# Expert loop of a mixture-of-experts layer: another order of the small products around gate/up and down

## What is computed

```python
logits = (t @ router_w + router_b)
top_val, top_idx = lax.top_k(logits, TOP_K)      # 4 of 32 experts for each token
gates = softmax(top_val)
for each expert e, for its tokens:
    g, u = split(x @ w_gu[e] + b_gu[e])          # w_gu[e]: 1024 x 2048
    act = (clip(u, -7, 7) + 1) * (min(g, 7) * sigmoid(1.702 * min(g, 7)))
    y = act @ w_down[e] + b_down[e]              # w_down[e]: 1024 x 1024
    out[token] += gate * y
```

## Time and profile before

| | |
|---|---|
| runs | 1322.9, 1323.15, 1326.55 us; median 1323.15 |
| profiled execution | 1325.46 us, of it the span 1323.7 us |
| granted TensorE clock, mean | 0.996 of full |
| TensorE busy | 1265.5 us, 96% |
| TensorE weight load | 583.3 us, 44% |
| VectorE busy | 544.5 us, 41% |
| ScalarE busy | 178.2 us, 13% |
| read from HBM | 476.10 MB |
| chain that ended last | PE 72%, DMA 21%, VectorE 5% |

### The profile page before, as it was taken

One profiled execution on the slowest core, in us unless ns is written; L12 is line 12 of the kernel. 1 busy time (PEld: TensorE's weight loads), 2 busy tenths in 40 slices (PEclk: granted clock), 3 DMA queues, 4 the chain that ended last, 5 costly groups with the idle time before them and its releaser, 6 DMA issues.

```text
span 1323.7 us, 16748 instructions
## 1 busy us (share of the span) xinstructions
PE 1265.5 (96%) x5959; PEld 583.3 (44%) x5960; DVE 544.5 (41%) x1166; ACT 178.2 (13%) x378; POOL 12.5 (1%) x31
## 2 busy tenths in 40 slices
PE   6999999999999999999989999999999999899997
PEld 4877866888653333333333333333333333233332
DVE  3244687332154334443343344334344343334344
ACT  2101323331020011000110000001000011001002
POOL 0000000110000000000000000000000000000000
PEclk9999999999999999999999999999999999999999
DMA  9957665337668999999999999999999999799995
GB/s 355 324 206 290 228 231 191 127 127 287 237 243 353 429 428 428 428 428 429 428 430 429 428 428 429 428 428 428 426 429 428 430 428 428 307 432 428 429 428 212
DMA packets 59182, 477.53 MB, mean 361 GB/s; under 512 B 4991, under 2 KB 5076, under 8 KB 32532
## 3 DMA queue, kind: packets, MB, share of 16 engines
q1 hardware_dynamic: 58852, 476.11, 87.4%
q10 hardware_dynamic: 304, 1.06, 0.2%
HBM read 476.10 MB, written 1.05 MB: 360 GB/s over the span
## 4 chain that ended last, share of the span: by engine, by line
PE 72%; DMA 21%; DVE 5%; issue 2%; ACT 1%; SPq 0%; DVEq 0%; ACTq 0%
PE bank L1727 23%; DMA down_ring<-in_w_down 17%; PE bank L1764 15%; PE bank L1365 11%; PE bank L1555 4%; PE bank L1715 3%; PE bank L1693 3%; DMA gu_ring<-in_w_gu 3%; PE bank L1454 2%; PE bank L1400 2%; PE bank L1618 2%; PE bank L1685 2%; DVE scratch L1200 1%; DVE scratch L1198 1%; DMA xres<-in_x 1%
## 5 line engine op out<-in xcount | busy, mean ns | idle before, releaser
L1727 PE MATMUL bank<-gu_ring,scratch 128*64 128x512 f32 x2048 | 461.2, 597 | 2.2 <-DVE scratch L1130 1.6
L1727 PEld LDWEIGHTS bank<-gu_ring,scratch 128*64 128x64 f32 x2048 | 143.6, 137 | 286.9 <-issue 285.4
L1764 PE MATMUL bank<-down_ring,scratch 128*64 128x512 f32 x1024 | 233.8, 598 | 23.7 <-DMA down_ring<-in_w_down 18.5
L1365 PE MATMUL bank<-gu_ring 128*128 128x256 f32 x640 | 143.8, 381 | 0.0
L1764 PEld LDWEIGHTS bank<-down_ring,scratch 128*64 128x64 f32 x1024 | 70.5, 136 | 144.9 <-issue 132.3
L1365 PEld LDWEIGHTS bank<-gu_ring 128*128 128x128 f32 x640 | 119.8, 190 | 20.3 <-issue 4.0
L1188 DVE TENSOR_TENSOR scratch<-bank,bgu 128x512 f32<-128x512 f32 x32 | 22.1, 692 | 220.2 <-PE bank L1693 220.2
L734 ACT ACTIVATE scratch<-bank 128x512 f32<-128x512 f32 x32 | 19.1, 597 | 685.9 <-PE bank L1727 685.9
L1156 DVE TENSOR_TENSOR xres<-xres,bank 128x512 f32<-128x512 f32 x132 | 81.9, 683 | 59.5 <-PE bank L1715 59.5
L1693 PEld LDWEIGHTS bank<-ident,scratch 128*128 128x128 f32 x392 | 41.1, 140 | 79.5 <-ACT scratch L734 26.0
L1129 DVE TENSOR_TENSOR scratch<-bank,a 128x512 f32<-128x512 f32 x33 | 22.8, 692 | 115.0 <-PE bank L1693 115.0
(11 more groups left out here) (271 smaller groups left out, 830.9 us busy)
## 6 DMA issues: line engine op xcount, KB each, us to landing
gu_ring<-in_w_gu SPq DMA_DIRECT2D x128, 2048.0 KB, 24.7
down_ring<-in_w_down SPq DMA_DIRECT2D x64, 2048.0 KB, 17.7
gu_ring<-in_w_in SPq DMA_DIRECT2D x32, 1024.0 KB, 8.8
gu_ring<-in_w_ada SPq DMA_DIRECT2D x16, 1024.0 KB, 7.0
down_ring<-in_w_ada SPq DMA_DIRECT2D x8, 512.0 KB, 10.5
gu_ring<-in_w_ada SPq DMA_DIRECT2D x8, 512.0 KB, 11.5
gu_ring<-in_w_pa SPq DMA_DIRECT2D x4, 1024.0 KB, 6.3
gu_ring<-in_w_pb SPq DMA_DIRECT2D x4, 1024.0 KB, 6.3
```

Source lines behind the costliest of these rows:

```text
L1365: last = M(dst[:, b * T:(b + 1) * T], group_chunk(group, kt // 4)[:, kt % 4, cols], hT[:, kt, :], start=kt == 0, stop=kt == KT - 1)
L1727: last = M(bank[f // 2][64 * a:64 * a + 64, :], xT[:, kt % 4, kt // 4, :], gu_ring[:, 8 * half + kt, f * 512:(f + 1) * 512], start=kt == 0 ...
L1764: last = M(bank[7][64 * a:64 * a + 64, :], act_sb[:, kt % 4, kt // 4, :], down_ring[:, kt // 2, (kt % 2) * D + a * 512:(kt % 2) * D + (a + ...
```

## The change

Seen from TensorE, item n's order becomes: gate/up with the transposes of gate inside as before and nothing else in it; both tiles of take; the transposes of up; way_back; take_transposed; the further passes; give of item n - 1; all down products in one run. Give now writes banks 0, 1, 2 and 4, so that the next expert's gate/up waits for VectorE's additions (given_added), and VectorE makes them at the end of its item, behind take. One memset adds one to given_added ahead of the loop, so that all its counts rise by one. ScalarE's copy of the way back comes behind the further passes and waits for give (given_done), which still reads the former one. A further pass uses banks 1 and 3 where it used 5 and 6, waits for act_ready before bank 3, and ends with a new wait of TensorE for f_added.

```diff
--- before.py
+++ after.py
@@ -375,6 +375,7 @@
             return 38 + n
 
         TURN_G2B = 42
+        GIVEN = (0, 1, 2, 4)
         EMPTIED_HT = KT
 
         block = ctx.enter_context(nc.Block())
@@ -713,6 +714,8 @@
             def copy_back(item):
 
                 act.wait_ge(back_done, item + 2)
+                if not isinstance(item, int):
+                    act.wait_ge(given_done, item * 4 + 4)
                 A(back[:], bank[5][:, 0:T], ACT.Copy).then_inc(back_ready, 1)
 
             def by_pairs(columns):
@@ -737,15 +740,15 @@
                 act.wait_ge(gu_used, item * 8 + 8)
                 A(in_blocks(u_raw), by_fours(bank[1][:, :]), ACT.Copy).then_inc(raw_ready, 1)
                 copy_taken(item + 1)
+                further_passes(act, item, count, further)
                 copy_back(item)
-                further_passes(act, item, count, further)
 
             def further(b, k):
 
                 act.wait_ge(f_taken, k + 1)
                 A(in_blocks(f_x), bank[4][:, 0:2 * P].rearrange("s (p r) -> s r p", r=2), ACT.Copy).then_inc(f_xraw, 1)
                 act.wait_ge(f_back_done, k + 1)
-                A(f_back, bank[5][:, 0:T], ACT.Copy).then_inc(f_back_ready, 1)
+                A(f_back, bank[1][:, 0:T], ACT.Copy).then_inc(f_back_ready, 1)
                 act.wait_ge(f_gu_done, k + 2)
                 A(in_blocks(g_raw), by_fours(bank[0][:, :]), ACT.Copy).then_inc(f_raw, 1)
                 act.wait_ge(f_gmin, k + 1)
@@ -766,7 +769,7 @@
 
             for n in range(4):
                 tt, half = n // 2, slice(n % 2 * 512, (n % 2 + 1) * 512)
-                act.wait_ge(given_added, NE * 4 + n + 1)
+                act.wait_ge(given_added, NE * 4 + n + 2)
                 A(xn[:, 1, half] if tt else scratch[:, half], xres[:, tt, half], ACT.Square, accum_out=osq[:, n:n + 1]
                   ).then_inc(sq_done, 1)
                 if n == 2:
@@ -1142,6 +1145,7 @@
             V.tensor_scalar(passes[:, 2, :], passes_f[:, 1, :], 1.0, None, ALU.add)
             V.tensor_copy(passes[:, 0:2, :], passes_f[:]).then_inc(passes_ready, 1)
             take(0)
+            V.memset(small[:, 4:5], 0.0).then_inc(given_added, 1)
 
             dve.wait_ge(bdown_in, 32)
             dve.wait_ge(emptied, EMPTIED_HT + TURN_G2B + 1)
@@ -1153,7 +1157,7 @@
                     tt, half = n // 2, n % 2
                     cols = slice(half * 512, (half + 1) * 512)
                     dve.wait_ge(given_done, item * 4 + (n + 5))
-                    V.tensor_tensor(xres[:, tt, cols], xres[:, tt, cols], bank[4 + n][:, :], ALU.add
+                    V.tensor_tensor(xres[:, tt, cols], xres[:, tt, cols], bank[GIVEN[n]][:, :], ALU.add
                                     ).then_inc(given_added, 1)
 
             def further_pick(expert, first, made):
@@ -1179,7 +1183,6 @@
                             own.then(last)
                 last.then_inc(gated_ready, 1)
                 pick(item + 1)
-                add_given(item - 1)
                 count = further_count(dve, item)
                 before_it = dve.value_load(passes[0:1, 1, bass.ds(item, 1)], min_val=0, max_val=T * TOPK // FCAP)
                 further_pick(item, pass_start[:, 0:1], item + before_it)
@@ -1201,6 +1204,7 @@
                                            ).then_inc(act_ready, 1)
                 further_passes(dve, item, count, lambda b, k: further(item, b, k))
                 take(item + 1)
+                add_given(item - 1)
 
                 dve.wait_ge(down_used, item * 2 + 2)
                 V.tensor_tensor(y_sb, bank[7][:, :], g2b, ALU.mult).then_inc(y_ready, 1)
@@ -1221,7 +1225,7 @@
                 def by_quarters(t):
                     return t.rearrange("p (q c) -> p c q", c=2).unsqueeze(3).to_broadcast([P, 2, 4, FCAP])
 
-                taken = bank[6][:, 0:KT * FCAP].rearrange("p (c q s) -> p c q s", c=2, q=4)
+                taken = bank[3][:, 0:KT * FCAP].rearrange("p (c q s) -> p c q s", c=2, q=4)
                 raw = bank[2][:, :].rearrange("p (j f s) -> p j f s", j=4, f=4)
                 g, u, sg = g_sb[:, :, :, 0:FCAP], u_sb[:, :, :, 0:FCAP], sig[:, :, :, 0:FCAP]
                 dve.wait_ge(act_ready, expert * 2 + 2)
@@ -1712,13 +1716,14 @@
                 for n in range(4):
                     tt, a = n // 2, n % 2
                     rows_ = slice(64 * a, 64 * a + 64)
-                    M(bank[4 + n][:, :], back[rows_, tt * P:(tt + 1) * P], y_sb[rows_, :], start=True, stop=True
+                    M(bank[GIVEN[n]][:, :], back[rows_, tt * P:(tt + 1) * P], y_sb[rows_, :], start=True, stop=True
                       ).then_inc(given_done, 1)
 
             def expert(item, half, fills):
 
                 count = further_count(pe, item)
                 pe.wait_ge(xTe_ready, item + 1)
+                pe.wait_ge(given_added, item * 4 + 1)
 
                 def gate_up(kt, parts):
 
@@ -1739,23 +1744,19 @@
                         gate_up(kt, range(4))
                     else:
                         gate_up(kt, (0, 1))
-                    if kt == 1:
-                        give(item - 1)
                 gate_up(KT - 3, (2, 3))
                 pe.wait_ge(raw_ready, item * 2 + 1)
                 transposes(2, g_raw).then_inc(gT_done, 1)
                 gate_up(KT - 2, (2, 3))
                 gate_up(KT - 1, (2, 3))
-                pe.wait_ge(given_added, item * 4 + 4)
-                take(item + 1, (0,))
+                take(item + 1)
                 pe.wait_ge(raw_ready, item * 2 + 2)
                 transposes(3, u_raw).then_inc(uT_done, 1)
-                take(item + 1, (1,))
                 way_back(item)
+                take_transposed(item + 1)
                 further_passes(pe, item, count, lambda b, k: further(item, half, fills, k))
+                give(item - 1)
                 for kt in range(KT):
-                    if kt == KT // 2:
-                        take_transposed(item + 1)
                     if kt % (KT // 2) == 0:
                         pe.wait_ge(act_ready, item * 2 + (1 + 2 * kt // KT))
                     if kt % 4 == 0:
@@ -1778,14 +1779,15 @@
                                  skip_group_check=True)
                 last.then_inc(f_taken, 1)
                 pe.wait_ge(f_gated, (expert + k) * 2 + 2)
-                pe.wait_ge(back_ready, expert + 2)
+                pe.wait_ge(raw_ready, expert * 2 + 2)
                 for tt in range(TT):
-                    last = nc.tensor.transpose(bank[5][:, tt * P:(tt + 1) * P],
+                    last = nc.tensor.transpose(bank[1][:, tt * P:(tt + 1) * P],
                                                f_gates[:, tt, :, :].rearrange("p a s -> p (a s)"), ident[:])
                 last.then_inc(f_back_done, 1)
                 pe.wait_ge(f_xraw, k + 1)
+                pe.wait_ge(act_ready, expert * 2 + 2)
                 for c in range(2):
-                    last = nc.tensor.transpose(bank[6][:, c * P:(c + 1) * P], f_x[:, c * P:(c + 1) * P], ident[:])
+                    last = nc.tensor.transpose(bank[3][:, c * P:(c + 1) * P], f_x[:, c * P:(c + 1) * P], ident[:])
                 last.then_inc(f_takenT, 1)
                 pe.wait_ge(f_mark, k + 1)
                 pe.wait_ge(f_xT_ready, k + 1)
@@ -1815,6 +1817,7 @@
                     rows_ = slice(64 * a, 64 * a + 64)
                     M(bank[n][:, :], f_back[rows_, tt * P:(tt + 1) * P], f_y[rows_, :], start=True, stop=True
                       ).then_inc(f_given, 1)
+                pe.wait_ge(f_added, k * 4 + 4)
 
 
             take(0, (0,), early=True)
```

## The result

The changed kernel takes 1332.3 us (median of 10 executions, 1330.07 to 1338.45) against 1324.41 us on the same chip (10 executions, 1321.67 to 1328.49): ratio 1.0059, 95% interval 1.0046 to 1.0073, so 7.8 us slower by the ratio. The forecast was +2.6 us with an upper end of +6.6: the sign was named, the size was not.

What follows compares the result with a forecast made beforehand. Weights were taken to bound the middle experts (29.37 us against TensorE's 27.38) and TensorE the further pass. The terms -1.2 (start), +4.0 (pass) and -0.2 (end) summed to +2.6 us, 1325.8 us on the median; range 1321.0 to 1329.8.

Steps and rivals of the forecast that it cites:

- (c): Expert 25's further pass, from the last awaited weights' landing to the next load request: 4.0 us longer (3.6 to 5.1).
- What bounds the kernel: Expert loop: weights lead at 29.37 us per expert, TensorE at 27.38 elsewhere; TensorE is the chain in the further pass.
- (a): Ordinary expert: same products in fewer groups, 26.7 us against 27.38 where TensorE leads, 0.7 us less, added waits covered.
- The rival that let this gain reach the end: Some 22 experts: fewer pattern changes pay everywhere, -11.4 us, 1311.7 us; chance 0.04.
- (b): Start of the weight stream: two requests for expert 2's weights issued 1.9 us sooner, -1.2 us (-1.6 to 0).
- clock rival: Products behind two waits for weights: TensorE's granted clock falls, 3.7 us more, +6.3 in all, 1329.5 us; chance 0.12.
- (d): From the load request behind the further pass to the end: weights eat the last experts' gain, -0.2 us (-0.3 to +0.3).
- exit case: Start and further pass's end: the start gains nothing and the loops' exit costs 2.0, +4.9 us, 1328.1 us; chance 0.10.

Runs made afterwards that it cites:

- gradual order of loads: Changed kernel, SP asking for three of expert 27's gate/up pairs ahead of down(26), down halves moved forward over experts 26 to 29: ratio 1.0019.
- give_first: Changed kernel with give(item - 1) and its additions ahead of the further pass, without the wait for f_added at its end: ratio 1.003, 1328.22 us.

## Why the prediction was right in sign and wrong in size

The step that failed is (c), what the further pass adds between L and D: 4.0 us were forecast and 9.9 came. Three terms of it were wrong: the loops' exit, taken at 1.1 and measured at 3.09; the start of the pass, 0.2 and 0.86; and TensorE's clock behind the gaps, counted at nothing and 3.2 us in the profiled execution. Together they are 5.9 us, which is what the sum lacks there (8.5 against 2.6). Of the signs it had named, one of being wrong came true (the clock fell below 1.00 in the loop) and one of being right came out too large (the silence of the DMA is 16 us, not 10); the 29.4 us per expert in the middle and the DMA piece ahead of expert 31's last products are as it said.

*What bounds the kernel* was read rightly. The weights lead in the middle; the end hangs on the further pass and the restart of the stream. The runs without the pass show it: 1.2 us between the kernels.

*(a), an ordinary expert at 26.7 instead of 27.38 us*: measured 26.48. The waits said to be covered are: in the trace of the changed kernel neither act nor the additions hold TensorE in an ordinary expert. Laid side by side with the earlier trace rows, the chains say where the 0.90 us lie. The gate/up products take 13.89 us for 14.03 (give no longer stands among them), down in one run 7.02 for 3.65 + 3.58. The transposes of the taken rows take 0.55 for 0.59. From 496.33 to 497.89 the kernel before needs 1.56 us for take's second half, the way_back transposes and 0.19 of waiting for VectorE; the same work takes 0.86 + 0.22 = 1.08 now. So 0.19 is a wait that has gone and some 0.7 is time at changes from one kind of product to another, of which an expert now has five fewer; no run varied these changes alone. The Trainium skill (TensorEngine Tiling, Tiling Modes) says that a change of tiling mode drains TensorE, and the direction of these pieces agrees. The rival that let this gain reach the end (1311.7) did not happen: where the weights lead it buys nothing.

*(b), the start*: -1.6 for -1.2. The two requests leave SP at 400.74 and 405.89 us, 8.82 and 13.97 behind S where they were 10.83 and 15.97 behind it: 2.0 us sooner, 1.9 was forecast. The stretch at 303 GB/s is gone (426 and 438 between 400 and 408 us).

*(c), the further pass*. "That 0.86 is the loop's exit, of which more may be hidden under the products; behind the new wait it is exposed. I take 1.1 (0.9 to 2.0)." The exit is 3.09, and it is the loops' (0.36 without them). At the entry the prediction looked at bank 3 and at the wait for ScalarE's copy and not at the loops. TensorE had waited 0.43 us for that copy, which is now done before TensorE gets there, and instead it shows 1.04 us of issue (0.35 without the loops). In the +6.3 of the table lie the wait for the additions (0.76, as forecast), the exit (3.09 for 1.1), the later start of the pass (0.86 for 0.2: 0.61 of a longer gap and 0.25 of work that moved ahead of it) and the clock in the down products (5.24 for 3.68, 1.56, for nothing). The clock is in give too (3.24 for 1.92) and in down's first half (0.3). The upper bound of 2.0 had no row behind it, and no row could have given one, because TensorE's branch instructions are not in the profile as work. The clock's three pieces make the 3.2 us.

*The clock rival* had the right mechanism, one right place of two and too little weight. It was put at 0.12 and at 3.7 us, with two falls behind waits for weights. The one behind expert 31's last pair came (1.7 us), the one behind L did not in this execution (2.79), and the falls in the pass, 3.2 us, were not among them. "Against it: a wait of 2.62 us in the pass left the clock at 1.00": the changed kernel has the same wait of 2.62 us and the clock falls behind it, and so it does once in the kernel before with another order of loads. One execution with no fall was taken for a bound. The wait of 2.10 us ahead of an expert's last gate/up pair shows in a single execution how weak such a bound is; the timeline at experts 23 and 25:

```profile
1047.62 4.49 PE L1732 MATMUL bank<-gu_ring,scratch 128*64 128x512 f32 x12 [2.10 <-DMA gu_ring<-in_w_gu]
...
1106.36 2.79 PE L1732 MATMUL bank<-gu_ring,scratch 128*64 128x512 f32 x12 [2.10 <-DMA gu_ring<-in_w_gu]
```

The same wait, the same products: once 4.49 us and once 2.79. The Trainium skill (TensorE: Matmul & The Clock Gate, Part 1: The HAM clock gate) says that the gate judges activity by a window that runs free of the kernel, so that the point at which the clock changes varies from run to run. The two rows agree with it in so far as the same wait ends either way. Falls in the gaps of the pass are 3.2 of the 5.9 us that the sum lacked in the profiled execution.

*(d), from D to the end*: 168.6, where 168.3 was worked out and 168.1 taken. That is luck in part, as two errors cancel: the last gate/up pair lands at D + 149.6 instead of 150.75, and the fall of the clock behind it costs 1.7. That the weights eat the last experts' gain is shown by the gradual order of loads, which gives some 5 us back.

*The range* ended at 1329.8, where one rival alone stood. The exit case (0.10; its own terms add up to +4.7, not +4.9) and the clock (0.12) were taken as separate. They are not: the longer gap at the exit had half clock behind it in all four executions that show it, and with the gap gone (give ahead of the pass) down ran at full clock. Added up, the two rivals reach the measured time.

What single cures give back (5.6 us the clock, 5.3 the order of loads, 3.8 give ahead of the pass, each uncertain by some 2.5) comes to more than the 7.8: they are not shares. The shorter exit of give_first brought the full clock with it, and the order of loads also takes away the fall at expert 31. The runs show that each helps, and not how the loss divides in the medians.

What stays open: where the clock is lost in the executions with the lower mean, why the same gap is followed by a fall once and not another time, and the stall of 5.35 us where the longer code of the pass is stepped over. It was seen in one version's expert 1, one of 1.32 us in another's, and no run looked into either.

## What to carry to other kernels

A wait added at the end of a loop or branch body can cost more than what it waits for: here it uncovered TensorE's own branch and loop instructions, which no busy time shows (3.09 us for 0.86), and queued behind it were give, the down products and the next request for weights. Where TensorE stands idle for some 2 us, as here, in a chain that leads to the end, one execution at full clock is no bound; count the fall at its price and with a good chance, or fill the gap. And before moving work out of a stretch that transfers lead into one that the engine leads, note that its price changes from nothing to all of it.

## What was not expected of the hardware

- The same 2.10 us without TensorE work ahead of the same products is followed by half clock in some cases and not in others, in one execution (4.49 and 2.79 us for 12 instructions); the same 2.62 us in six of twelve profiled executions. It needs no change of order either: behind the same 1.92 us, ahead of 16 down instructions near 875 us, these take 3.65 us in the kernel before and 5.35 in the same kernel with only the later loads reordered. In the ten executions of the changed kernel the mean granted clock goes from 0.991 to 0.985, and the time from 1330 to 1338 us.
- The exit of two nested loops and their branches takes TensorE 3.1 us behind a wait and shows 0.86 us beside running products; with a plain branch in their place it is 0.36 us and nothing.
- With 28 more products in a branch that 31 of 32 experts step over, TensorE stood 5.35 us once, in expert 1, at the place where it is stepped over, and not in the others. With 12 more there was one stall of 1.32 us, in expert 1's down products, and with 6 more none. That the added code is the cause is not shown.
